# Mixture-of-experts stage of a two-part network: token blocks of 32 on quarters of the array instead of 64 on halves

## The chip, the cores and the metric

The kernel runs on one core of a Trainium2 chip. Engines by the profile's names: PE is the matrix engine (TensorE), PEld its weight loads, DVE the vector engine, ACT the scalar engine, POOL GpSimd, SP the engine that here only issues transfers. The metric is the device time of one execution in microseconds (us); lower is better. Before the change, three executions took 3697.03, 3705.31 and 3705.87 us, median 3705.31.

## The reference

The reference is a long float32 network for 512 tokens of 1024 channels: a recurrent token mixer with a Fourier branch, a mixture of experts, and two attention layers. Only the mixture of experts is touched:

```python
logits = h @ w_router + b_router                  # 512 tokens, 32 experts
top_val, top_idx = lax.top_k(logits, 4)           # each token goes to 4 experts
# for each expert e and the tokens that chose it:
u = xb @ w1[e] + b1[e]                            # 1024 -> 2048
glu = jnp.minimum(u[:, 0::2], 7.0)
lin = jnp.clip(u[:, 1::2], -7.0, 7.0)
act = glu * jax.nn.sigmoid(1.702 * glu) * (lin + 1.0)
y = act @ w2[e] + b2[e]                           # 1024 -> 1024
```

The gates weight the four results of a token and they are summed. One expert's w1 is 8 MB and its w2 is 4 MB, so the stage reads 402.65 MB of weights. The 2048 assignments are spread over the experts very unevenly. With the reference's own inputs and router, experts 0 to 31 get 44, 173, 113, 53, 8, 58, 162, 39, 48, 26, 50, 21, 51, 17, 79, 21, 70, 52, 73, 42, 159, 35, 36, 87, 96, 69, 135, 57, 66, 55, 46 and 7 tokens.

## The kernel before

**Routing (`settle`, from line 1386).** DVE turns the router's result into a count per expert (lines 1553 to 1558), a rank of every assignment within its expert, and a list that says which token stands in which row of which block (lines 1566 to 1577; the last product, on PE, is line 1477). `nblki` holds the number of blocks of each expert, one more than the number of multiples of 64 that its count exceeds. Here that makes 48 blocks. This chain is serial, and nothing of the expert stage's PE work starts before its list is there.

**The expert stage (`experts`, from line 1589).** A block is up to 64 tokens (`HT`) of one expert. All weights are loaded in pieces of 1 MB (line 1621, SP's queue) into a ring of 20 places (`RING`); an expert is 12 pieces, eight of w1 and four of w2, in the order of use. Nine of the first pieces are already loaded during `settle`, eleven more when the stage starts (line 1625). Piece n+20 is asked for when piece n has been used for the last time, that is in the last block of its expert (`used`, line 1620). A piece of w1 is two groups of 128 rows by one half of the columns, with runs of 4 KB.

For each block PE does, in this order: two bias products (line 1685, one ahead of each half of the first layer), 8 pieces of the first layer and 4 of the second (line 1698), two turns of the activations (line 1704) and one turn of the next block's rows (lines 1672 and 1674). A piece is four matmuls of 512 columns in float32. The tokens are the stationary operand, 64 columns wide, so that two matmuls run side by side on the two column halves of the array. The trace shows each float32 matmul as two instructions, so a block has 96 instructions of line 1698. DVE forms the activation (`swiglu`, lines 1791 to 1798) for one half while PE works on the next pieces. ACT computes the sigmoid and copies everything that is turned (lines 1748 to 1774), then writes the block's result with two transfers (line 1744). POOL gathers the next block's rows by their indices (line 1643), after PE has turned the present ones (`turned`), and makes the selector of the bias (line 1652).

Loops run over experts and, within them, over the expert's number of blocks, which each engine reads from `nblki` (line 1608). Whether the block is an expert's first or a later one, it runs the same instructions and the same waits. Within a block the second layer stands behind the first of the same block.

After the stage, `combine` (from line 1805) gathers four result rows for each token.

Of the kernel before, what the change touches and what calls it, by code (L numbers as in the profile page):

```python
# [57 lines left out]
MAXB = 64  # L58


def constants():
# [11 lines left out]
        "edges": np.broadcast_to(64.0 * np.arange(1, 9)[None, :], (P, 8)),  # L73
        "token": P * np.arange(TT)[None, :] + p,
        "headrow": (p % 32) == np.arange(8)[None, :],
        "halves": (p // 64) == (f // 64),
# [1309 lines left out]
def settle(nc, A, ps, T, R, M, N, spill, rows_in, raw_in, stored, kmt):  # L1386
# [6 lines left out]
    with stage(nc, "b_in", "var_ready", "root_ready", "scaled", "normed", "taken", "h_ready", "kept", "saved", "turned", "ht_out", "high", "pool_step",  # L1393
# [20 lines left out]
        def _(pool):  # L1414
# [9 lines left out]
            for i in (1, 3):  # L1424
                lo = slice(E * i, E * i + E)
                done(pool.tensor_tensor(M["b12"][lo, :], N["b1r"][lo, :], M["b12"][lo, :].bitcast(F32), ALU.subtract))

        @block.tensor
        def _(pe):
# [46 lines left out]
            for j in range(JK):  # L1476
                last = pe.matmul(ps[0:64, 7, 0:MAXB], R["who"][:, j, :], R["where"][:, j, :], start=(j == 0), stop=(j == JK - 1))
# [3 lines left out]
        def _(act):  # L1481
# [17 lines left out]
            act.activation(M["b12"][:, :], N["b1r"][:, :], ACT.Copy).then_inc(high, 1)  # L1499
# [10 lines left out]
        def _(dve):  # L1510
# [55 lines left out]
            done(dve.scalar_tensor_tensor(out=R["row"][:, :], in0=R["blk"][:, :], scalar=64.0, in1=R["rank"][:, :], op0=ALU.mult, op1=ALU.add))  # L1566
            done(dve.tensor_copy(T["slot"][:, :], R["row"][:, :]))
            done(dve.tensor_tensor(R["over"][:, 0:JK, :], bc(R["rank"][:, :], 2, 8), bc(S("edges"), 1, JK), ALU.is_ge))
            done(dve.tensor_reduce(R["low"][:, :], R["over"][:, 0:JK, :], AX_X, ALU.add))
            done(dve.tensor_tensor(R["blk"][:, :], R["blk"][:, :], R["low"][:, :], ALU.add))  # L1570
            done(dve.scalar_tensor_tensor(out=R["low"][:, :], in0=R["low"][:, :], scalar=-64.0, in1=R["rank"][:, :], op0=ALU.mult, op1=ALU.add))
# [7 lines left out]

def piece_source(A, e, s):  # L1580

    w1 = A["w1"][0, e].rearrange("(k p) n -> p k n", p=P)
    w2 = A["w2"][0, e].rearrange("(k p) n -> p k n", p=P)
    if s < 8:
        return w1[:, 2 * (s % 4):2 * (s % 4) + 2, (s // 4) * D:(s // 4 + 1) * D]
# [1474 lines left out]
```

## Time and profile before

| | us |
|---|---|
| median of three executions (lowest, highest) | 3705.31 (3697.03, 3705.87) |
| span of the profiled execution | 3706.0 |
| expert stage on PE (first to last matmul of line 1698) | 979.6 to 2151 |
| PE busy over the span | 3295.0 (89%) |
| PE idle in the expert stage, waiting for weights | 27.2 |
| loads of 1 MB from w1 and w2 | 384 |
| mean transfer rate in most of the expert stage | 369 to 399 GB/s |

The page divides the span in 40 slices of 92.65 us; the expert stage is slices 11 to 24. In them PE is busy nearly all the time and DVE and ACT are nearly idle, while the transfer engines are at nine tenths or more in most slices. The profile's own execution stands at the median of the timed ones, so sums made against its span carry over.

### The profile page before, as it was taken

To read this page: it belongs to the slowest core of one execution; us is meant where nothing else is said; L and a number is where in the kernel's file an instruction comes from. 1 tells how busy PE (TensorE), PEld (TensorE's weight loads), DVE (VectorE), ACT (ScalarE), POOL (GpSimd) and SP (SyncE) were. 2 spreads that over 40 slices of the span, in tenths; PEclk is the share of its full clock that TensorE was granted. 3 is DMA by queue.
4 is the path that set the end of the run, shared out by engine and by line. 5 is a ranking of instruction groups with operands and counts; after the bars stand their busy time and mean duration, and the time that the engine had idled before them with its cause. 6 is when DMAs were issued, how large, how long until landed. Compare 5 with 4: busy or idle time off the path is not lost. (4 is left out here: it accounts for less than half of the span.)

```text
span 3706.0 us, 63217 instructions
## 1 busy us (share of the span) xinstructions
PE 3295.0 (89%) x25517; PEld 2108.3 (57%) x25518; DVE 1399.2 (38%) x2384; ACT 984.3 (27%) x1766; POOL 154.3 (4%) x221
## 2 busy tenths in 40 slices
PE   3998788787799997999999969987899899878998
PEld 2878677676433332333333327865578778655787
DVE  5535545546211111111111146544643365446433
ACT  2333313312111111111111103343532233435321
POOL 0000000000300000000000010000000000000000
PEclk8999889888799999999999989997999999979999
DMA  6621320324789999998986944331033133310331
GB/s 217 237 97 33 98 94 8 98 71 157 298 297 396 366 400 399 396 397 320 397 312 244 385 172 122 99 49 35 1 93 101 45 115 101 47 35 1 94 100 57
DMA packets 273124, 647.39 MB, mean 175 GB/s; under 512 B 36890, under 2 KB 97050, under 8 KB 270978
## 3 DMA queue, kind: packets, MB, share of 16 engines
q1 hardware_dynamic: 251314, 605.12, 45.6%
q0 software_dynamic: 6224, 21.24, 1.8%
q10 hardware_dynamic: 15360, 17.82, 1.5%
q8 instruction: 167, 2.74, 0.3%
q14 instruction: 59, 0.48, 0.0%
HBM read 600.85 MB, written 43.27 MB: 174 GB/s over the span
## 5 line engine op out<-in xcount | busy, mean ns | idle before, releaser
L1698 PE MATMUL ps<-raw,ex_xT 128*64 128x512 f32 x3072 | 698.0, 599 | 21.8 <-DMA raw<-in_w_dram 21.7
L1698 PEld LDWEIGHTS ps<-raw,ex_xT 128*64 128x64 f32 x3072 | 206.6, 137 | 419.2 <-issue 375.9
L1791 DVE TENSOR_SCALAR ex_gl<-ps 128x256 f32<-128x256 f32 x96 | 40.8, 425 | 1014.4 <-PE ps L1698 1014.4
L1698 PE MATMUL ps<-raw,ex_aT 128*64 128x512 f32 x1536 | 350.8, 596 | 6.1 <-DMA raw<-in_w_dram 5.5
L1698 PEld LDWEIGHTS ps<-raw,ex_aT 128*64 128x64 f32 x1536 | 105.3, 137 | 205.0 <-issue 187.5
L1950 PE MATMUL ps<-zhi,hh 128*128 128x512 f32 (+1 forms) x448 | 169.8, 379 | 0.4 <-DVE hl L2080 0.4
L1951 PE MATMUL ps<-zlo,hh 128*128 128x512 f32 (+1 forms) x448 | 169.0, 377 | 0.0
L1952 PE MATMUL ps<-zhi,hl 128*128 128x512 f32 (+1 forms) x448 | 168.6, 376 | 0.0
L2497 PE MATMUL ps<-uu_hi,hh 128*128 128x512 f32 x384 | 151.9, 395 | 12.2 <-DVE uu_lo L2609 12.2
L2499 PE MATMUL ps<-uu_hi,hl 128*128 128x512 f32 x384 | 152.2, 396 | 0.0
L2498 PE MATMUL ps<-uu_lo,hh 128*128 128x512 f32 x384 | 152.0, 396 | 0.0
L2609 DVE TENSOR_TENSOR uu_lo<-u_raw,uu_hi 128x2048 fp32r<-128x2048 f32 x30 | 68.6, 2292 | 202.7 <-ACT uu_hi L2575 202.7
L1765 ACT ACTIVATE ex_aT<-ps 128x256 f32<-128x256 f32 x96 | 36.8, 383 | 406.4 <-PE ps L1704 406.4
L2497 PE MATMUL ps<-uu_hi,u_oh 128*128 128x512 f32 x320 | 126.7, 396 | 0.4 <-DVE u_ol L2614 0.4
L2071 DVE TENSOR_TENSOR zlo<-oT,zhi 128x1024 fp32r<-128x1024 f32 (+1 forms) x64 | 74.6, 1166 | 137.2 <-ACT zhi L1987 136.5
L2498 PE MATMUL ps<-uu_lo,u_oh 128*128 128x512 f32 x320 | 126.3, 395 | 0.0
L2499 PE MATMUL ps<-uu_hi,u_ol 128*128 128x512 f32 x320 | 126.3, 395 | 0.0
L1987 ACT ACTIVATE zhi<-oT 128x1024 fp32r<-128x1024 f32 (+1 forms) x64 | 64.9, 1014 | 215.5 <-PE ps L1952 155.6
L1759 ACT ACTIVATE ex_arow<-ex_gl 128x256 f32<-128x256 f32 x96 | 40.0, 417 | 300.1 <-DVE ex_gl L1791 300.1
L2575 ACT ACTIVATE uu_hi<-u_raw 128x2048 fp32r<-128x2048 f32 x30 | 57.3, 1915 | 213.2 <-PE ps L2499 207.2
L2307 ACT ACTIVATE za<-ps,nsa_nm 128x256 f32<-128x256 f32 (+3 forms) x160 | 81.1, 511 | 109.0 <-DVE nsa_nm L2331 109.0
L2270 PE MATMUL ps<-small,za 128*128 128x128 f32 x544 | 86.1, 291 | 16.2 <-DVE za L2342 16.2
(558 smaller groups left out, 6018.8 us busy)
## 6 DMA issues: line engine op xcount, KB each, us to landing
raw<-in_w_dram SPq DMA_DIRECT2D x384, 1024.0 KB, 19.3
oT<-in_w_in_dram SPq DMA_DIRECT2D x64, 512.0 KB, 3.6
u_raw<-in_w_in_dram SPq DMA_DIRECT2D x24, 1024.0 KB, 5.2
expert_out<-xn SPq DMA_DIRECT2D x4, 4096.0 KB, 16.8
expert_out<-ex_yrow ACTq DMA_DIRECT2D x98, 128.0 KB, 6.4
late_ada<-in_w_ada_dram SPq DMA_DIRECT2D x12, 1024.0 KB
early_w<-in_w_in_dram SPq DMA_DIRECT2D x10, 1024.0 KB, 6.6
mT<-in_w_ada_dram SPq DMA_DIRECT2D x4, 2048.0 KB, 19.9
```

The costliest lines, as they stand in the source:

```text
L1698: mm = pe.matmul(o, x, M["raw"][:, (slot + LATE_SLOTS) % RING, k, h * 512:(h + 1) * 512], start=(s >= 8 and kk == 0), stop=(kk == 7))
L1950: pe.matmul(o, x_hi, w_hi, start=(kk == 0), stop=False)
L1951: pe.matmul(o, x_hi, w_lo, start=False, stop=False)
L1952: last = pe.matmul(o, x_lo, w_hi, start=False, stop=(kk == KD - 1))
L1987: act.activation(hi[q % nh][cut], raw[q % nr][cut], ACT.Copy).then_inc(hi_done, 1)
L2071: dve.tensor_tensor(lo[q % nh][cut], raw[q % nr][cut], hi[q % nh][cut].bitcast(F32), ALU.subtract).then_inc(lo_done, 1)
L2270: mm = pe.transpose(ps[:, 4 + x, b * P:(b + 1) * P], Z["p"][:, i % NB, x, b * P:(b + 1) * P], S("ident"))
L2307: act.activation(Z["p"][:, i % NB, x, 0:u["n"]], ps[:, (i % 2) * 2 + x, 0:u["n"]], ACT.Exp, bias=Z["nm"][:, i % 4, x:x + 1], accum_out=Z[" ...
L2497: pe.matmul(o, x_hi, w_hi, start=first, stop=False)
L2498: pe.matmul(o, x_hi, w_lo, start=False, stop=False)
L2499: return pe.matmul(o, x_lo, w_hi, start=False, stop=last)
L2609: dve.tensor_tensor(lo[q % nh], raw[q % nr], hi[q % nh].bitcast(F32), ALU.subtract).then_inc(lo_done, 1)
```

## The change

`HT` becomes 32: a block has up to 32 tokens, and its matmuls have 32 stationary columns and run on four column quarters. A first-layer piece is now one group of 128 rows of w1 with all 2048 columns (8 KB runs), four matmuls of 512 columns, one for each quarter, all into one bank. In the second layer a quarter takes 256 of the 1024 result columns: a piece is eight matmuls of 256 columns. Each expert has at least two blocks and otherwise one for each begun 32 tokens. PE's order changes too: first layer of block w, turn of block w-1's activations, turn of block w+1's rows, second layer of block w-1. An expert's first block is a copy of the code of its own, with the waits for the pieces; later blocks have none. `swiglu` and the sigmoid run once a block. The result goes out with four transfers of 32 rows by 256 columns instead of two of 64 by 512.

```diff
-MAXB = 64
+MAXB = 128
+HT = 32
+EDGES = SEQ // HT
@@ settle, SP @@
-            b1 = A["b1"][0].rearrange("e (p h n) -> h e p n", p=2, h=2)
-            for i in range(4):
-                sp.dma_start(N["b1r"][E * i:E * i + E, :].rearrange("e (p n) -> e p n", p=2), b1[i // 2]).then_inc(b_in, 16)
+            for j in range(4):
+                sp.dma_start(N["b1r"][E * j:E * j + E, :], A["b1"][0][:, j * 512:(j + 1) * 512]).then_inc(b_in, 16)
@@ settle, POOL @@
-            for i in (1, 3):
-                lo = slice(E * i, E * i + E)
-                done(pool.tensor_tensor(M["b12"][lo, :], N["b1r"][lo, :], M["b12"][lo, :].bitcast(F32), ALU.subtract))
+            done(pool.tensor_tensor(M["b12"][:, 1, :], N["b1r"][:, :], M["b12"][:, 0, :].bitcast(F32), ALU.subtract))
@@ settle, PE @@
-                last = pe.matmul(ps[0:64, 7, 0:MAXB], R["who"][:, j, :], R["where"][:, j, :], start=(j == 0), stop=(j == JK - 1))
+                last = pe.matmul(ps[0:HT, 7, 0:MAXB], R["who"][:, j, :], R["where"][:, j, :], start=(j == 0), stop=(j == JK - 1))
@@ settle, DVE (and HT, EDGES for 64 and 8 in the lines after) @@
-            done(dve.tensor_tensor(R["over"][:, :, :], bc(cnt, 2, 8), bc(S("edges"), 1, E), ALU.is_gt))
+            done(dve.tensor_tensor(R["over"][:, :, :], bc(cnt, 2, EDGES), bc(S("edges"), 1, E), ALU.is_gt))
             done(dve.tensor_reduce(R["nblk"][:, :], R["over"][:, :, :], AX_X, ALU.add))
+            done(dve.tensor_scalar(R["nblk"][:, :], R["nblk"][:, :], 1.0, None, ALU.max))
+            done(dve.tensor_copy(R["nblki"][:, 0, :], R["nblk"][:, :]))
             done(dve.tensor_scalar(R["nblk"][:, :], R["nblk"][:, :], 1.0, None, ALU.add))
-            done(dve.tensor_copy(R["nblki"][:, :], R["nblk"][:, :]))
+            done(dve.tensor_copy(R["nblki"][:, 1, :], R["nblk"][:, :]))
@@ piece_source @@
-    if s < 8:
-        return w1[:, 2 * (s % 4):2 * (s % 4) + 2, (s // 4) * D:(s // 4 + 1) * D]
-    return w2[:, 2 * (s - 8):2 * (s - 8) + 2, :]
+    if s < 8:
+        return A["w1"][0, e].rearrange("(k p) (a n) -> p k a n", p=P, a=2)[:, s, :, :]
+    return A["w2"][0, e].rearrange("(h k p) n -> p k h n", p=P, h=2)[:, s - 8, :, :]
@@ experts, SP: reload @@
-                    sp.wait_ge(used, w * NP + s + 1)
+                    if s < W1P:
+                        sp.wait_ge(used1, w * W1P + s + 1)
+                    else:
+                        sp.wait_ge(used2, w * W2P + s - W1P + 1)
@@ experts, PE @@
+            def bias(w):
+                pe.wait_ge(picked, w + 1)
+                pe.matmul(ps[:, WIDE, :], M["pick"][:, :], M["b12"][:, 0, :], start=True, stop=False)
+                pe.matmul(ps[:, WIDE, :], M["pick"][:, :], M["b12"][:, 1, :], start=False, stop=False).then_inc(bias_done, 1)
+            def first_layer(w, i, g, fresh):
+                pe.wait_ge(x_out, w + 1)
+                for s in range(W1P):
+                    if fresh:
+                        landed(i, g + s)
+                    for j in range(4):
+                        mm = pe.matmul(ps[HT * j:HT * j + HT, WIDE, :], M["xT"][:, s, :], M["raw"][:, place((g + s) % NS), j // 2, (j % 2) * 512:(j % 2) * 512 + 512],
+                                       start=False, stop=(s == W1P - 1))
+                    mm.then_inc(used1, 1)
+            def second_layer(w, i, g, fresh):
+                pe.wait_ge(y_out, w + 1)
+                pe.wait_ge(at_out, w + 1)
+                for s in range(W2P):
+                    if fresh:
+                        landed(i, g + W1P + s)
+                    for half in range(2):
+                        for n in range(4):
+                            mm = pe.matmul(ps[HT * n:HT * n + HT, OUT, 0:256], M["aT"][:, 4 * half + s, :],
+                                           M["raw"][:, place((g + W1P + s) % NS), half, n * 256:(n + 1) * 256],
+                                           start=(s + half == 0), stop=(s + half == W2P))
+                    mm.then_inc(used2, 1)
+            def one_block(i, g, before, fresh):
+                w = now()
+                pe.wait_ge(emptied, w)
+                bias(w)
+                first_layer(w, i, g, fresh)
+                turn_act(w - 1)
+                turn_rows(w + 1)
+                second_layer(w - 1, i, before, before == g)
+                pe.reg_add(r, r, 1)
+            def expert(i, e, g):
+                one_block(i, g, g - NP, True)
+                with pe.Fori(0, later_blocks_of(pe, e)) as _:
+                    one_block(i, g, g, False)
@@ experts, ACT @@
-                for h in range(2):
-                    act.dma_start(rows_out[bass.ds(at_row, HT), h * 512:(h + 1) * 512], M["yrow"][HT * h:HT * h + HT, :]).then_inc(written, 16)
+                for n in range(4):
+                    act.dma_start(rows_out[bass.ds(at_row, HT), n * 256:(n + 1) * 256], M["yrow"][HT * n:HT * n + HT, :]).then_inc(written, 16)
+            def body():
+                w = now()
+                act_out(w)
+                rows_turned(w + 2)
+                sigmoid(w + 1)
+                rows_back(w)
+                act.reg_add(r, r, 1)
```

## Rows read from the trace of the kernel before

**Rows 1.** Stretches of the expert stage: length, busy us (instructions), granted clock, transfer share, rate
```profile
core 0: us, PE busy (x) PEld busy (x) DVE busy (x) ACT busy (x) POOL busy (x), PEclk, DMA share, GB/s
1100.00:1200.00 100.00, 100.00 (x472) 33.92 (x468) 12.99 (x32) 17.59 (x29) 6.07 (x12) 1.00 1.02 388
...
1400.00:1500.00 100.00, 82.62 (x356) 24.17 (x354) 11.37 (x28) 12.65 (x22) 4.95 (x10) 0.98 1.03 399
```
**Rows 2.** Waits from 980 to 2150: who for whom, us in total, times, longest
```profile
PE ps L1698 <- DMA raw<-in_w_dram: 27.2, 40, 2.0
```
**Rows 3.** PE in order of time, one undisturbed block: start us, us, group, count
```profile
1568.24 0.51 PE L1685 MATMUL ps<-ex_b,ex_pick 128*128 128x512 f32 x1
1568.68 5.37 PE L1698 MATMUL ps<-raw,ex_xT 128*64 128x512 f32 x24
1573.98 0.44 PE L1704 MATMUL ps<-small,ex_arow 128*128 128x128 f32 x2
...
1576.11 3.60 PE L1698 MATMUL ps<-raw,ex_aT 128*64 128x512 f32 x16
1579.65 0.44 PE L1704 MATMUL ps<-small,ex_arow 128*128 128x128 f32 x2
...
1584.40 0.50 PE L1685 MATMUL ps<-ex_b,ex_pick 128*128 128x512 f32 x1
```
**Rows 4.** Weight loads in order of time where matmuls of 32 columns run on quarters
```profile
412.75 0.13 PEld L1149 LDWEIGHTS ps<-late_ada,cpad 128*32 128x32 f32 x4 [0.30 <-issue]
413.18 0.13 PEld L1149 LDWEIGHTS ps<-late_ada,cpad 128*32 128x32 f32 x4 [0.30 <-issue]
```
**Rows 5.** PE in order of time, quarters with only 128 columns
```profile
2535.01 0.27 PE L2142 MATMUL ps<-oT,za 64*32 64x128 f32 x2
...
2535.12 0.27 PE L2142 MATMUL ps<-oT,za 64*32 64x128 f32 x2
```
**Rows 6.** Costliest PE groups by line: busy us, mean ns, idle before
```profile
L2287 PE MATMUL ps<-za,zb 128*64 128x128 f32 x960 | 79.7, 301 | 0.0
```
**Rows 7.** Transfer queues from 1500 to 1600: packets, MB, share of 16 engines
```profile
q1 hardware_dynamic: 9767, 37.65, 96.2%
q0 software_dynamic: 320, 1.05, 3.9%
q10 hardware_dynamic: 640, 1.05, 2.8%
```
**Rows 8.** The same from 104 to 108, packets of 17 KB
```profile
DMA packets 96, 1.67 MB, mean 418 GB/s; under 512 B 0, under 2 KB 0, under 8 KB 0
```
**Rows 9.** PE in four stretches of 5 us: length, busy, granted clock, transfer share, rate
```profile
1425.00:1430.00 5.00, 2.96 (x12) 0.89 1.04 349
1430.00:1435.00 5.00, 4.74 (x18) 0.77 1.04 401
...
1440.00:1445.00 5.00, 4.12 (x20) 1.00 1.03 412
```
**Rows 10.** Routing's end in order of time
```profile
953.76 0.42 DVE L1553 TENSOR_TENSOR rt_over<-ps,small 128x256 f32<-128x256 f32 x1 [0.85 <-PE ps L1469]
...
954.89 0.18 DVE L1556 CAST nblki<-rt_nblk 128x32 int32<-128x32 f32 x1
...
962.48 1.23 DVE L1575 TENSOR_TENSOR rt_where<-small,rt_blk 128x1024 f32<-128x1024 f32 x1
963.76 3.67 PE L1477 MATMUL ps<-rt_where,rt_who 128*64 128x64 f32 x32 [9.26 <-DVE rt_where L1575]
```
**Rows 11.** Gather of the block's rows, POOL in order of time
```profile
1582.02 0.94 POOL L1643 DMA_INDIRECT ex_xrow<-expert_in,ex_index  x1 [0.77 <-POOL ex_index L1649]
```
**Rows 12.** The same gathers, from issue to landing, over the stage
```profile
DMA to landing us min/median/max: 3.6/6.9/8.1
```
**Rows 13.** ACT around a block's turns and its writes
```profile
1580.12 0.38 ACT L1765 ACTIVATE ex_aT<-ps 128x256 f32<-128x256 f32 x1 [2.92 <-PE ps L1704]
...
1584.51 0.60 ACT L1774 ACTIVATE ex_yrow<-ps 128x512 f32<-128x512 f32 x1 [3.00 <-PE ps L1698]
```

More of the change, by code:

```diff
@@ L72, in constants @@
         "causal": np.where(f <= p, 0.0, NEG),
-        "edges": np.broadcast_to(64.0 * np.arange(1, 9)[None, :], (P, 8)),
+        "edges": np.broadcast_to(float(HT) * np.arange(1, EDGES + 1)[None, :], (P, EDGES)),
         "token": P * np.arange(TT)[None, :] + p,
         "headrow": (p % 32) == np.arange(8)[None, :],
-        "halves": (p // 64) == (f // 64),
+        "quarters": (p // 32) == (f // 32),
         "eye32": (p % E) == np.arange(E)[None, :],
@@ L1498, in _ @@
             act.wait_ge(b_in, 64)
[L1499 removed]
+            act.activation(M["b12"][:, 0, :], N["b1r"][:, :], ACT.Copy).then_inc(high, 1)
             act.wait_ge(logit, 1)
@@ L1592, in experts, with counter, later_blocks_of, every_block_but_one @@
     NP, NS, EU = 12, RING, RING // int(np.gcd(RING, 12))
-    HT = 64
-    TURNED, ROWS_T = 5, 3
-    WIDE = (0, 1)
-    OUT = 2
-    with stage(nc, "used", "indexed", "picked", "bias_done", "turned", "x_out", "biased", "mixed", "sig", "acted", "at", "at_out",
+    W1P, W2P = 8, 4
+    TURNED, ROWS_T, WIDE, OUT = 5, 3, 0, 2
+    with stage(nc, "used1", "used2", "indexed", "picked", "bias_done", "turned", "x_out", "biased", "emptied", "mixed", "sig", "acted", "at", "at_out",
                "y_out", "written") as (
-            block, used, indexed, picked, bias_done, turned, x_out, biased, mixed, sig, acted, at, at_out, y_out, written):
-        def counter(eng, name, first=0):
+            block, used1, used2, indexed, picked, bias_done, turned, x_out, biased, emptied, mixed, sig, acted, at, at_out, y_out, written):
+        def counter(eng, name):
             r = eng.alloc_register(name)
-            eng.reg_mov(r, first)
-            return r, lambda top=MAXB - 1: eng.snap(r, min_val=first, max_val=top)
+            eng.reg_mov(r, 0)
+            return r, lambda top=MAXB - 1: eng.snap(r, min_val=0, max_val=top)
         def blocks_of(eng, e):
-            return eng.value_load(R["nblki"][0:1, bass.ds(e, 1)], min_val=1, max_val=SEQ // HT)
+            return eng.value_load(R["nblki"][0:1, 1, bass.ds(e, 1)], min_val=2, max_val=EDGES)
+        def later_blocks_of(eng, e):
+            return eng.value_load(R["nblki"][0:1, 0, bass.ds(e, 1)], min_val=1, max_val=EDGES - 1)
+        def every_block_but_one(eng, body):
+            with eng.Fori(0, later_blocks_of(eng, 0)) as _:
+                body()
+            with eng.Fori(1, E) as e:
+                with eng.Fori(0, blocks_of(eng, e)) as _:
+                    body()
+        def place(slot):
+            return (slot + LATE_SLOTS) % RING
         @block.sync
@@ L1662, in _ @@
             r, now = counter(pe, "pe_blocks")
-            pe.sem_inc(used, NP)
             pe.sem_inc(turned, 1)
@@ L1731, in _ @@
-            turn_rows(0)
-            with pe.Fori(0, E // EU) as i:
-                for j in range(EU):
-                    expert(i, j)
-            for j in range(E % EU):
-                expert(E // EU, j)
+            def bias(w):
+                pe.wait_ge(picked, w + 1)
+                pe.matmul(ps[:, WIDE, :], M["pick"][:, :], M["b12"][:, 0, :], start=True, stop=False)
+                pe.matmul(ps[:, WIDE, :], M["pick"][:, :], M["b12"][:, 1, :], start=False, stop=False).then_inc(bias_done, 1)
@@ new lines, in turn_act @@
+            def turn_act(w):
+                pe.wait_ge(acted, w + 1)
+                for i2 in range(2):
+                    mm = pe.transpose(ps[:, ROWS_T, i2 * P:(i2 + 1) * P], M["arow"][:, i2 * P:(i2 + 1) * P], S("ident"))
+                mm.then_inc(at, 1)
+            def second_layer(w, i, g, fresh):
[10 more added lines that the diff above has]
+                    mm.then_inc(used2, 1)
@@ new lines, in _ @@
+            turn_rows(0)
+            bias(0)
+            first_layer(0, 0, 0, True)
+            turn_rows(1)
+            pe.reg_add(r, r, 1)
+            with pe.Fori(0, later_blocks_of(pe, 0)) as _:
+                one_block(0, 0, 0, False)
+            whole = (E - 1) // EU
+            with pe.Fori(0, whole) as i:
+                for j in range(EU):
+                    expert(i, i * EU + (j + 1), NP * (j + 1))
+            for e in range(1 + whole * EU, E):
+                expert(0, e, NP * e)
@@ L1738, in _ @@
+            w = now(MAXB)
+            turn_act(w - 1)
+            second_layer(w - 1, 0, NP * (E - 1), False)
         @block.scalar
```

169 lines of the change are left out of this document (61 added, 108 removed).

## Prediction

> **What bounds the kernel now.** I read the page's slices first: the expert stage is slices 11 to 24 of 40, with PE at nine tenths or ten and the transfer engines nearly as full. So two things compete, and the stretches of the stage say which one wins where [rows 1]: from 1100 to 1200 PE is busy 100.00 of 100 us at full clock with 388 GB/s beside it; from 1400 to 1500 it is busy 82.62 us while the transfer share is 1.03 and the rate 399 GB/s. The first kind of stretch is PE-bound, the second is load-bound. The waits give the sum: in all, PE sat idle for weights for only 27.2 us [rows 2]. The stage lasts 979.6 to 2151 = 1171.4 us. The change touches this stage and the end of routing; everything after is the same code.
>
> One block, from one bias product to the same one of the next block, runs from 1560.79 to 1584.40 = 23.61 us; the rows show its later part [rows 3]. Matmuls of line 1698 come in pairs on the two halves, 4 instructions in 0.857 us (24 from 1568.68 to the turn at 1573.98, 5.30 us, of which about 0.16 is filling). So 96 instructions take 20.57 us. The rest, 3.04 us, is the array emptied and filled again around other shapes: a bias product 0.59 each (twice), the first turn 0.53, the second turn with the row turn 1.32. 48 blocks x 23.61 = 1133.3 us, and 1171.4 - 1133.3 = 38 us is what waiting adds (27.2 of it plainly idle, the rest refilling and the slow clock at a few waits).
>
> The loads: from 1500 to 1600 with four blocks [rows 7], the shares of the queues add to 102.9%. The weight queue's part is 96.2 / 102.9 = 93.5 us for 37.65 MB, 2.60 us for a piece of 1 MB. A block's gather and write take (3.9 + 2.8) / 102.9 / 4 = 1.63 us; I use 1.67, as the stretch of 1400 to 1500 gives. An expert of one block takes the loads 12 x 2.60 + 1.67 = 32.9 us, PE 23.6.
>
> **A check of how the two combine.** I carry two sums through the 32 experts with the counts of the reference: loads one after another, no piece before the one 20 places earlier was used in its expert's last block; PE block by block, no first-block piece before it has landed. With the numbers above this gives an end of PE at 2151.6 (the trace: 2151), 38.7 us of waiting, and 107 us in which the loads stand because the ring is full. The long experts (3 blocks, 71 us of PE against 35 of loads) fill the ring and stop the loads; the run of short ones after them empties it and PE waits, above all at experts 11 to 14. I use the same two sums for the change.
>
> **PE's work per block.** First layer: 32 matmuls are 64 instructions, 4 at a time on quarters. The trace has this shape: 4 weight loads every 0.43 us with matmuls of 512 columns [rows 4]. 16 x 0.429 = 6.86 us, half of the 13.7 of before, for half the tokens. Second layer: 64 instructions of 256 columns, which no row shows. From below, quarters with 128 columns come 4 in 0.11 us [rows 5], so streaming, not issue, sets the pace, and 256 columns should take 0.214 for 4: 3.43 us. From above, matmuls of 128 columns on halves cost 79.7 / 960 = 0.083 us each where streaming alone would be 0.053 [rows 6]; at 0.083 each the layer is 5.3 us. I take 3.43, since rows 5 have the same quarters. Bias: one excursion, 0.59 + 0.22 for the second product = 0.81. Turns: one excursion, 1.32 as before, since line 1674 is issue-bound and not shortened. Sum 0.81 + 6.86 + 1.32 + 3.43 = 12.42 us for 32 tokens.
>
> **Blocks.** Counts up to 64 give two blocks, also the six experts with 32 or fewer; ceil(count / 32) beyond. Sum 87. PE: 87 x 12.42 = 1080.5 us against 1133.3, 52.8 less. Experts of one block go from 23.6 to 24.8, those with 65 to 96 tokens (seven) from 47.2 to 37.3, expert 2 (four blocks) from 47.2 to 49.7, the four of three blocks from 70.8 to 62.1 (five) or 74.5 (six).
>
> **What could wait within 12.42 us.** The second layer needs the turned activations: ACT's copy ended 0.85 us after the turn began [rows 3, 13], and the row turn covers 1.16. The gather follows the row turn: it is issued 2.4 us after the turn of the activations began and takes at most 8.1 to land [rows 3, 11, 12], 10.5 in all, and the next row turn begins 0.4 + 12.4 = 12.8 after; half as many rows. If this cover were gone, each us beyond would cost 87 us less the 49 of waiting. ACT issues four writes instead of two, about 2.3 us after the copy of the result [rows 13], with the next turn 7 us away. SP's queue waits for the second layer of an expert's last block, which now stands behind the next expert's first-layer pieces; these 8 are in the ring already (12 + 8 = 20), so it is 4 pieces late by one first layer and the sums hold it. I cost all of these at nothing.
>
> **Loads.** A w1 piece has runs of 8 KB in place of 4. Packets of 17 KB moved 1.67 MB in 4 us, 418 GB/s [rows 8]; the weight queue does 37.65 / 93.5 = 403. I take 2.50 us for a w1 piece (419 GB/s), 2.60 for w2; the bounds are 2.60 and 2.45. Gather and write per block: half the bytes but smaller writes; 0.9 us, from 0.7 to 1.3. An expert of two blocks: 8 x 2.50 + 4 x 2.60 + 1.8 = 32.2 us against PE's 24.8.
>
> **The clock.** Before, a starved PE had its waits spread over all 12 pieces. A wait of 2.04 us near 1426 took the granted clock to 0.89 and 0.77 in the next stretches, while waits of some 0.6 us each left it at 1.00 [rows 9]. Now a piece is used in 0.86 us and lands every 2.5, so a starved first layer waits 1.6 us at each piece: I expect 1.2 GHz there and 3 us more per such expert (bounds 0 and 5), nine times, 27 us.
>
> **The sum.** The two sums with these numbers: PE 1080.5, waiting 48.8, clock 27, the last second layer's turn 1.2: 1157.5 us against 1172.0, so -14.5. Where the ring is empty (experts 9 to 14) the stage goes at the loads' 32.2 us an expert; where five or six blocks come (1, 6, 20, 26, also 2) PE falls behind and the loads stand for 115 us. That is where the saved PE time goes: the floor by the loads alone would be some 115 us lower.
>
> Routing's end is on the path [rows 10]: the list product gets 128 moving columns instead of 64 at half clock, 3.67 to about 6.9 (+3.2); `rt_where` doubles (+1.1), the two `rt_who` steps halve (-1.2), the edges double (+0.8), two small operations (+0.4): +4.4. Two more writes at the end +1, more code to fetch +1. Total -14.5 + 6.4 = -8.1: span 3697.9, and since the span stands 0.7 above the median, 3697.
>
> **One rule against it.** The weight loads of the four quarters overlap each other and the matmuls: 4 of them take 0.13 us and recur every 0.43, which is streaming alone [rows 4]. By the Trainium skill, "TensorE: Matmul & The Clock Gate", Part 3, a weight load overlaps running matmuls only when its row group differs, and column quarters share theirs. The trace disagrees. Taken at its word it would add 0.13 to each of 32 groups of a block, rival B with 4.2 us.
>
> **Rivals.**
> A, loads gain nothing and starve PE as now: w1 pieces at 2.60. The stage then is 1178.9, +6.9; total +13: 3719. For: the steady rate may be a limit of all 16 engines. Against: rows 8.
> B, slower: a group of quarters doesn't reach streaming pace in the second layer. At 5.3 us the block is 14.3, PE 1244 with hardly a wait left: stage +90, 3800. It decides from about 0.5 us a block, where the two sums give no gain at all. For: rows 6, and 4.2 us by the rule gives more, near 4000. Against: rows 5.
> C, faster: the clock holds and block traffic is small (0.8, w1 2.45, block 12.1): stage -46, 3665. For: waits of 0.6 us left it at 1.00. Against: 2.04 did not.
> D, the gather lands over 2.3 us later than its longest or another hand-over is late, 1 us a block: stage +28, 3740. Against: rows 12.
>
> **Chances.** Forecast 0.44, A 0.20, B 0.08, C 0.16, D 0.12. What this kernel's measurement can tell from no change is about 0.3%, 11 us: below 3694 is faster, above 3716 slower. Half of the forecast's own range (3680 to 3714) is below 3694. Faster: half of 0.44 + C, and a little of A: 0.41. Slower: B, D, over half of A: 0.29. Same 0.30. The range reaches from C to D: 3662 to 3748.
>
> **What would show it.** Right: 87 blocks; bias to bias 12.4 us where nothing waits; second-layer weight loads 4 in 0.21; PE busy near 1080 us of the stage and waiting 50 to 75; clock under 1.00 at experts 9 to 14; slices above 410 GB/s. Wrong: a period of 14 (B), idle on the gather or on ACT's copy (D), the weight queue still at 403 (A), clock at 1.00 throughout (C).

## The result, and the profile after

The changed kernel takes 3733.0 us (median of four executions, 3728.2 to 3739.7) against 3705.6 us for the kernel before on the same chip: ratio 1.0074, 95% interval 1.0062 to 1.0087. The forecast was 3697. The profiled execution's span is 3734.3 us, against 3706.0.

The stage, from the first bias product to the end of the last second-layer matmul, lasts 1197.8 us (983.98 to 2181.8) against 1172.2 (978.78 to 2151.0): +25.6 of the +28.3 us by which the spans differ. The rest, +2.7, lies outside the stage. When the stage starts differs by up to 18 us between the profiled executions of the kernels below (965.6 to 984.0), and that difference is already there at routing's `rt_over` (937.0 to 957.0). So below I compare the stage's length, not where it ends.

The same two stretches as in [rows 1], changed kernel:

```profile
1100.00:1200.00 100.00, 97.19 (x1108) 40.45 (x1104) 12.84 (x32) 11.66 (x32) 11.64 (x24) 1.00 0.88 340
1400.00:1500.00 100.00, 84.20 (x862) 31.68 (x858) 9.63 (x24) 8.75 (x24) 8.89 (x18) 0.90 1.02 401
```

The kind of stretch is as before, but the granted clock of the second is 0.90 for 0.98. PE from 1046 on, one undisturbed block to hold against [rows 3]:

```profile
1046.85 0.50 PE L1694 MATMUL ps<-ex_b,ex_pick 128*128 128x512 f32 x1
...
1047.52 7.07 PE L1708 MATMUL ps<-raw,ex_xT 128*32 128x512 f32 x64
1054.53 0.44 PE L1716 MATMUL ps<-small,ex_arow 128*128 128x128 f32 x2
...
1055.66 3.66 PE L1728 MATMUL ps<-raw,ex_aT 128*32 128x256 f32 x64
1059.25 0.50 PE L1694 MATMUL ps<-ex_b,ex_pick 128*128 128x512 f32 x1
```

Bias to bias is 12.40 us; the forecast had 12.42. The 64 second-layer instructions run in 3.6 us, the forecast's streaming pace (3.43) and some filling. There are 87 blocks; at 12.40 each they are 1078.8 us of PE. So the work of PE is what was forecast. The waits of PE in the stage are not:

```profile
PE ps L1708 <- DMA raw<-in_w_dram: 33.3, 30, 1.8
PE ps L1694 <- issue: 29.0, 5, 6.0
PE ps L1708 <- issue: 12.3, 5, 2.5
```

The first line answers to [rows 2] (27.2 before). The two "issue" lines have no counterpart there: ten idle times in which PE waited for nothing that the profile shows, five ahead of a bias product and five within the first layer behind it. This is PE in order of time around the first pair:

```profile
1198.88 0.50 PE L1694 MATMUL ps<-ex_b,ex_pick 128*128 128x512 f32 x1
...
1207.69 3.66 PE L1728 MATMUL ps<-raw,ex_aT 128*32 128x256 f32 x64
1217.40 0.79 PE L1694 MATMUL ps<-ex_b,ex_pick 128*128 128x512 f32 x1 [6.05 <-issue]
1217.98 0.63 PE L1695 MATMUL ps<-ex_b,ex_pick 128*128 128x512 f32 x1
1218.54 1.94 PE L1708 MATMUL ps<-raw,ex_xT 128*32 128x512 f32 x8
1222.92 9.02 PE L1708 MATMUL ps<-raw,ex_xT 128*32 128x512 f32 x56 [2.44 <-issue]
...
1236.59 0.50 PE L1694 MATMUL ps<-ex_b,ex_pick 128*128 128x512 f32 x1
```

The block before takes 1217.40 - 1198.88 = 18.52 us and the next 19.19, for 12.40 each: 12.9 us more, of which 8.5 are the two idle times and 4.4 the slower clock after them (8 matmuls in 1.94 us instead of 1.07). The other four pairs stand at 1414, 1586, 1785 and 1960; measured in the same way they cost 11.6, 12.1, 11.9 and 11.7 us. These five places are where PE's outer loop over five experts turns back. Together that is some 60 us of PE's time (the expectations below take 12.9 for each, the largest of the five); part of it comes back, since the loads go on meanwhile.

What is transferred in the stage (985 to 2150) by the instruction queue, packets of 16 KB, kernel before first, then changed:

```profile
q8 instruction: 6, 0.10, 0.0%
```

```profile
q8 instruction: 83, 1.36, 0.5%
```

I read this so: the kernel before brings its loop's instructions once and keeps them, and the changed one brings them again at each turn. The queue's row doesn't say which engine its packets are for; the experiments decide. The changed kernel's PE loop holds, for each of five experts, the block twice (the first block with waits for its pieces, and a later one), ten copies of 282 matrix instructions and weight loads (64 + 64 + 13 pairs of them); before it was five copies of 222.

The weight queue from 1500 to 1600 [rows 7]:

```profile
q1 hardware_dynamic: 6836, 38.59, 96.2%
q10 hardware_dynamic: 1325, 0.90, 2.8%
q0 software_dynamic: 288, 0.79, 2.5%
```

With the 0.6% of the instruction queue the shares add to 102.1; the weight queue's part is 94.2 us for 38.59 MB, 410 GB/s; from 1400 to 1500 the same working gives 407. Before it was 403. A piece is 2.56 to 2.58 us on average; the forecast had 2.53 (2.50 for w1). A block's gather and write are 5.3 / 102.1 of 100 us over about six to seven blocks, 0.8 us; the forecast had 0.9.

Routing's end [rows 10], and the stage's last turn of the activations on ACT and PE:

```profile
965.91 2.29 DVE L1576 TENSOR_TENSOR rt_where<-small,rt_blk 128x2048 f32<-128x2048 f32 x1
...
968.26 5.79 PE L1476 MATMUL ps<-rt_where,rt_who 128*32 128x128 f32 x32 [10.48 <-DVE rt_where L1576]
```

```profile
2172.99 0.44 PE L1716 MATMUL ps<-small,ex_arow 128*128 128x128 f32 x2
2173.21 0.38 ACT L1791 ACTIVATE ex_yrow<-ps 128x256 f32<-128x256 f32 x1 [3.01 <-PE ps L1728]
2173.77 1.75 ACTq L1773 DMA_DIRECT2D expert_out<-ex_yrow  x4
2175.92 0.38 ACT L1786 ACTIVATE ex_aT<-ps 128x256 f32<-128x256 f32 x1 [2.32 <-issue]
...
2176.45 5.35 PE L1728 MATMUL ps<-raw,ex_aT 128*32 128x256 f32 x64 [3.01 <-ACT ex_aT L1786]
```

At the very end no next block's work stands between the turn and the second layer. ACT copies the result, issues four writes (1.75 us) and only then copies the turned activations: PE waits 3.0 us and then runs for a while at the slower clock (5.35 us for 3.66), 4.7 us in all.

### The profile page after: what moved, and what is told of

Same layout as the page of the kernel before. It is cut to its first block and busy times, and to the rows that moved or that the text cites. A ratio compares the mean times of both kernels' runs of the same rounds, so it can differ in the third digit from the quotient of the medians.

```text
span 3734.3 us, 78487 instructions
## 1 busy us (share of the span) xinstructions
PE 3274.6 (88%) x32456; PEld 2181.9 (58%) x32457; DVE 1383.1 (37%) x2350; ACT 916.2 (25%) x1779; POOL 206.7 (6%) x337
## 5 line engine op out<-in xcount | busy, mean ns | idle before, releaser
L1708 PE MATMUL ps<-raw,ex_xT 128*32 128x512 f32 x5568 | 649.6, 615 | 45.6 <-DMA raw<-in_w_dram 33.3
L1708 PEld LDWEIGHTS ps<-raw,ex_xT 128*32 128x32 f32 x5568 | 173.9, 112 | 474.4 <-issue 403.6
L1728 PE MATMUL ps<-raw,ex_aT 128*32 128x256 f32 x5568 | 321.5, 383 | 3.0 <-ACT ex_aT L1786 3.0
L1728 PEld LDWEIGHTS ps<-raw,ex_aT 128*32 128x32 f32 x5568 | 173.0, 110 | 113.3 <-issue 5.8
L1791 ACT ACTIVATE ex_yrow<-ps 128x256 f32<-128x256 f32 x87 | 33.5, 385 | 266.1 <-PE ps L1728 266.1
```

Source lines behind the costliest of these rows:

```text
L1708: mm = pe.matmul(ps[HT * j:HT * j + HT, WIDE, :], M["xT"][:, s, :], M["raw"][:, place((g + s) % NS), j // 2, (j % 2) * 512:(j % 2) * 512 + ...
L1728: mm = pe.matmul(ps[HT * n:HT * n + HT, OUT, 0:256], M["aT"][:, 4 * half + s, :], M["raw"][:, place((g + W1P + s) % NS), half, n * 256:(n ...
```

## Experiments

The theory, F: the copies of PE's loop are too many bytes to be kept, so each turn back fetches them again and PE stands while the first come in. Its first rival, J: turning back costs in this loop whatever it holds. Each run's ratio is against the kernel before, measured beside it.

### PE's outer loop taken away

```diff
-            whole = (E - 1) // EU
-            with pe.Fori(0, whole) as i:
-                for j in range(EU):
-                    expert(i, i * EU + (j + 1), NP * (j + 1))
-            for e in range(1 + whole * EU, E):
+            for e in range(1, E):
                 expert(0, e, NP * e)
```

> The changed kernel with PE's 31 later experts written out one after another instead of six turns of a loop over five experts; the work is the same. Theory F (code fetch): the loop body, ten block copies, is some 180 KB of PE code and is not kept, so each of the five backward branches waits for its first code: the trace after shows 5 idle times of about 6.0 us and 5 of about 2.4 us, put down to issue, and slow clock behind them, 12.9 us a time against the 12.4 us period. Written out there is no backward branch over a long body: these idle times go, the time falls by 25 to 35 us (part of 64 us comes back as waits for weights) to about 3705, the code fetched stays near 86 packets in the stage. Rival G (the gaps are hand-overs of another engine, or the selector or gather at an expert's border): the gaps stay, 3733. Rival H (fetching any new code is the cost, not the branch): the time stays or rises, with the idle spread over all experts.

3708.2 us (3703.8 to 3714.8, ten executions), ratio 1.0008 [0.9998, 1.0017]; the stage is 1175.2 us, 22.6 shorter than in the changed kernel. Waits of PE in the stage, then its instruction queue:

```profile
PE ps L1708 <- DMA raw<-in_w_dram: 45.1, 40, 1.9
...
PE ps L1728 <- ACT ex_aT L1782: 3.0, 1, 3.0
```

```profile
q8 instruction: 72, 1.18, 0.4%
```

No wait for issue is left, though nearly as many instructions are fetched (72 packets for 83): in a straight line they are fetched ahead of PE. It is not the traffic that costs, but the standing still at the turn. The rivals G and H fall: the other engines and the work are the same, and the gaps are gone. Of the 41.3 us of idle time taken away, 11.8 come back as waits for weights. From 1400 to 1500, with no turn of the outer loop in it, the stretch is this:

```profile
1400.00:1500.00 100.00, 86.06 (x826) 30.26 (x822) 9.64 (x24) 8.72 (x24) 8.88 (x18) 0.85 1.02 403
```

Slower by 0.74% became slower by 0.08%: 24 us, the whole measured loss within the intervals. 1.18 MB for 62 copies of the block (those of all experts but the first) is about 19 KB for a copy, 67 bytes for each of its 282 instructions; by the same figure a copy of the kernel before is about 15 KB. My expectations say 18 and 14. Both are estimates: the packets may hold other engines' code too, and some of PE's may have come before 985. So every size below is given from the smaller figure to the larger.

### The turn back announced to the sequencer

```diff
-            with pe.Fori(0, whole) as i:
+            with nc.Fori(0, whole, engines=[mybir.EngineType.PE], hint_back_edge=True) as i:
```

> The changed kernel with a prefetch hint for the backward branch of PE's loop over five experts, nothing else. Theory F: the first code of the body is fetched before the branch, so the 6.0 us gaps shrink; the second gap of 2.4 us may stay. Between 3705 and 3720. Rivals G and H: 3733.

3727.4 us (3712.5 to 3732.9, five executions), ratio 1.0064 [1.0046, 1.0083]. In the profiled execution, the fastest of the five:

```profile
PE ps L1708 <- DMA raw<-in_w_dram: 33.8, 30, 2.1
PE ps L1708 <- issue: 16.4, 5, 4.1
PE ps L1694 <- issue: 9.1, 3, 3.2
```

The idle time falls from 41.3 to 25.5 us, the stage to 1187.1, and 81 packets are still fetched. The hint shortens the wait ahead of the bias product (9.1 us in all for 29.0), not the second one (16.4 for 12.3), and hardly a packet is saved. The median is above the 3705 to 3720 that I expected: this execution is 14 us faster than the next of the five, and the gain over the changed kernel is small, with intervals that overlap. So the run bears theory F out in what it does to the waits, not in the time.

### The kernel before, with ten experts in PE's loop instead of five

```diff
+    EP = 2 * EU
...
-            with pe.Fori(0, E // EU) as i:
-                for j in range(EU):
+            with pe.Fori(0, E // EP) as i:
+                for j in range(EP):
```

> The kernel before with PE's loop over ten experts a turn instead of five; the work is the same, the body grows from about 71 to 142 KB of code. Theory F: the body no longer stays, code packets in the stage rise from 6 to 30 or more, and the two backward branches (before experts 10 and 20) cost a gap of about 6 us each and slow clock: 13 us each of PE, of which the first is taken back from the waits for weights at experts 11 to 14: 3711 to 3720. Rival J (a backward branch by itself drains PE in the changed kernel, whatever the size of the body): the kernel before has five such branches without a gap, so this one has two fewer and stays at 3705.

3718.8 us (3713.5 to 3722.1, ten executions), ratio 1.0030 [1.0020, 1.0041]. Two rows of its waits, line 1686 being the bias product that opens the loop's body, and the instruction queue:

```profile
PE ps L1699 <- DMA raw<-in_w_dram: 25.2, 39, 2.1
...
PE ps L1686 <- issue: 7.8, 2, 3.9
```

```profile
q8 instruction: 32, 0.52, 0.2%
```

Fewer turns back, yet slower: only the size of the body has changed, and with it appear the fetching and the waits that the kernel before doesn't have. J falls for this loop; for the changed kernel's own loop it is decided by the run with two experts below. Here a turn costs one wait of 3.9 us where I expected 6, less than the 8.5 of the changed kernel.

### w1 pieces in runs of 4 KB again

```diff
-                sp.dma_start(M["raw"][:, place(slot), :, :], piece_source(A, ...)).then_inc(raw_in[slot], 16)
+                for h in range(2):
+                    sp.dma_start(M["raw"][:, place(slot), h, :], piece_source(A, ...)[:, h, :]).then_inc(raw_in[slot], 16)
```

The same is done to the first loads, and PE waits for both halves of a piece.

> The changed kernel with each piece loaded by two transfers of 512 KB, so that w1's runs are 4 KB again as in the kernel before; 8 KB runs are what this leaves out. The prediction's term (2.50 us for a w1 piece instead of 2.60) says that this costs up to 20 us: 3745 to 3753. The trace after says 38.40 MB in 96.3 of 102.0 shares from 1400 to 1500, 2.58 us a piece on average against 2.60 before, so a rival says that the runs are worth almost nothing: 3733 to 3738.

3748.5 us (3744.5 to 3755.7, four executions), ratio 1.0118 [1.0097, 1.0140]: 16 us slower than the changed kernel. The weight queue from 1400 to 1500:

```profile
q1 hardware_dynamic: 10468, 38.11, 97.4%
```

With the shares of the other queues (2.5, 2.4, 0.6, 0.1) that is 403 GB/s, the rate of before, for 407. So giving up the changed kernel's loads costs 16 us. How much of it the longer runs are worth isn't shown: this run also doubles the number of transfers, of w2 pieces too, and I can't part the two.

### The writes of a block issued one turn later (on the flat kernel)

```diff
                 act_out(w)
-                rows_turned(w + 2)
+                act.wait_ge(y_out, w + 1)
+                write(behind() * HT)
+                act.reg_mov(q, r)
+                rows_turned(w + 2)
                 ...
-                act.wait_ge(y_out, w + 2)
-                write(w * HT)
```

> The experts of PE written out flat, as in the run without an outer loop, and one thing more: ScalarE no longer issues the four row stores of block w right after it copied them, but a turn later, behind its act_out. Everything is computed as before. In the changed kernel and in the flat one the last act_out stands behind the issue of four stores (1.75 us) and the last second layer waits 3.0 us for it (ScalarE ex_aT), at the slower clock. Theory T (tail on the path, nothing else touched): the 3.0 us wait is under 0.5 us, stage from its first first-layer matmul 3 to 5 us shorter, 3704 us against 3708 of the flat one. Rival U (ScalarE's queue is needed mid stage): rows_turned, now behind the stores, comes 1.75 us later each block, x_out is waited for by PE in the blocks that do not wait for weights, a new wait 'ACT ex_xT' of up to 20 times 1 us, 3710 to 3725.

3700.3 us (3692.5 to 3712.1, twelve executions), ratio 0.9987 [0.9974, 0.9999]. The wait for ACT's copy is 1.1 us for 3.0, the stage 1171.4 us for 1175.2: 3.8 less, and no new wait appears mid stage. Theory T holds, though the wait isn't under 0.5 us as I expected of it: I take the remaining 1.1 us for the copy itself and the hand-over to it, as in an undisturbed block, where the turn of the rows covers it. The time is 8 us below the flat kernel's, more than the stage's 3.8, with intervals that just overlap.

### Experts of one block (with the late writes, flat)

```diff
-            done(dve.tensor_scalar(R["nblk"][:, :], R["nblk"][:, :], 1.0, None, ALU.max))
...
-                with pe.Fori(0, later_blocks_of(pe, e)) as _:
-                    one_block(i, g, g, False)
+                more = later_blocks_of(pe, e, 0)
+                pe.reg_mov(left, more)
+                with pe.If_ne(left, 0):
+                    with pe.Fori(0, more) as _:
+                        one_block(i, g, g, False)
```

PE's second layer now also has the waits for its pieces in every block, since the block before can be an expert's only one.

> The flat kernel with the late stores, and experts may have one block of 32 where they have at most 32 tokens; the changed kernel gives every expert at least two, so 6 of its 87 blocks are rows of nobody. Everything is computed. Theory G (PE's own time still bounds enough of the stage): 81 blocks in place of 87; by the recurrence over landings and blocks that fits the flat kernel the stage is 14 us shorter for it (not 6 x 12.4 = 74, since most of the removed blocks stand where PE waits for weights anyway), with the tail 3690 us. Rival H (the loads bound the stage where small experts stand): removed blocks turn into waits for weights one for one, 45 us of them become over 110 and the time is that of the run with late stores alone, 3704.

3686.0 us (3675.5 to 3696.7, six executions), ratio 0.9945 [0.9924, 0.9967]. The stage is 1156.8 us, 14.6 shorter than with late writes alone; 14 were expected for six blocks of 12.4 us less. Its waits:

```profile
PE ps L1708 <- DMA raw<-in_w_dram: 64.3, 55, 4.7
PE ps L1694 <- issue: 16.5, 4, 6.4
PE ps L1716 <- issue: 2.8, 1, 2.8
```

Theory G's numbers hold, and H's (over 110 us of waits, 3704) don't. Still, 60 of the 74 us are not gained. Of them 17 are more waits for weights and 19.3 are issue waits that come back; the rest is PE's slower clock and refilling, which no run parts (the granted clock from 1400 to 1500 is 0.76 for 0.85 in the flat kernel). The first of the issue waits:

```profile
1161.47 0.79 PE L1694 MATMUL ps<-ex_b,ex_pick 128*128 128x512 f32 x1 [6.02 <-issue]
```

This is the first block behind expert 4, which has 8 tokens, so that its copy for later blocks is jumped over. Counting blocks, the other three (at 1346.92, 1475.69 and 1551.47) stand behind experts 9, 13 and 15 and the one at line 1716 behind expert 31: five of the six experts with one block, and nowhere else. Behind expert 11 none is labelled so. A jump ahead over one copy can thus wait (1.4 to 6.4 us here) as a turn back does; that it waits for its instructions is the likely reading, but no run isolates it.

### The second layer between first-layer pieces 5 and 6

```diff
-                first_layer(w, i, g, fresh)
+                early = 6 if fresh else W1P
+                first_layer(w, i, g, fresh, range(early))
                 turn_act(w - 1)
-                turn_rows(w + 1)
+                if not fresh:
+                    turn_rows(w + 1)
                 second_layer(w - 1, i, before, True)
+                if fresh:
+                    first_layer(w, i, g, fresh, range(early, W1P))
+                    turn_rows(w + 1)
```

> As the kernel with one-block experts and late stores, and in an expert's first block PE does the second layer of the block before between pieces 5 and 6 of the first layer rather than behind piece 7. Everything is computed. PE waits for first-layer pieces in such blocks, 40 waits of about 1.1 us in the flat kernel; the second layer (3.66 us of work on pieces long there) would fill the wait for pieces 6 and 7. Theory W (waits in series with work that could fill them): 3 to 20 us shorter than the kernel without it. Rival X (loads bound): a second layer moved inside frees second-layer pieces a little earlier but first-layer pieces 6 and 7 3.7 us later, so the loads slip by as much as PE gains: within 3 us, or up to 5 longer since the turn of the rows also comes later and SwiGLU waits.

3677.6 us (3669.0 to 3686.8, six executions), ratio 0.9918 [0.9900, 0.9937]. The stage is 1151.3 us, 5.5 less than without it; the times differ by 8.4, with intervals that overlap. PE where it is starved:

```profile
1412.18 0.44 PE L1717 MATMUL ps<-small,ex_arow 128*128 128x128 f32 x2
1413.14 3.66 PE L1729 MATMUL ps<-raw,ex_aT 128*32 128x256 f32 x64 [0.52 <-issue]
1416.59 1.93 PE L1709 MATMUL ps<-raw,ex_xT 128*32 128x512 f32 x16
```

Pieces 6 and 7 (the last row, 16 matmuls) no longer wait: they landed during the second layer. In exchange a small wait stands ahead of it, 17.4 us over 32 blocks (0.5 us each). It is labelled "issue"; with no turn of the rows between, ACT's copy of the activations is what I take it for, but no row says so. Rival X's side shows too: PE waits for SwiGLU to empty the first layer's bank (5.9 us in 28 blocks, where there were 0.2), and for the next rows (13.0 us for 8.7). The small gain is on the side of theory W, at its low end. This is the fastest of all kernels run, 0.8% below the kernel before.

### How large a loop is kept

Four kernels place the limit. A loop over fewer experts needs the ring's used places to divide evenly, so the number of places changes with it; one line in the changed kernel sets both (places, experts in a loop; SP's loop over experts changes with it).

```diff
-    NP, NS, EU = 12, RING, RING // int(np.gcd(RING, 12))
+    NP, NS, EU = 12, 18, 3
```

> The changed kernel with its outer loop kept but the ring used to 18 places instead of 20, so that PE's loop holds three experts, not five: 6 block copies of about 18 KB of instructions, some 108 KB, where five experts are 180 KB. The loop turns back ten times, not five. Everything is computed. Theory F (code that is not there is fetched again at each turn only when the loop's body is too large to be kept): no waits for issue over 2 us at the branches, fewer than 25 instruction packets in the stage against 86. The two places fewer cost about 20 us by the recurrence of landings and blocks, so 3720 to 3735 us. Rival K (each backward branch of this loop costs, whatever the size): ten waits of 5 to 6 us, 20 us of places and 55 us of branches over the flat kernel, 3765 us or more.

3772.4 us (3765.6 to 3782.3, five executions), ratio 1.0178 [1.0157, 1.0198]. Here I was wrong, and the rival's number held:

```profile
PE ps L1694 <- issue: 51.1, 9, 5.9
PE ps L1708 <- DMA raw<-in_w_dram: 25.9, 24, 1.9
PE ps L1708 <- issue: 21.9, 9, 2.6
```

```profile
q8 instruction: 86, 1.41, 0.5%
```

Three experts in the loop, 108 to 114 KB, are not kept either. (The loop goes round ten times, so it turns back nine times, not ten.) Either the limit lies lower, or this kernel's loop is never kept. The next two differ only in the number of experts in the loop, two or three, at 12 places:

> The changed kernel with its outer loop kept, 12 places of the ring in use and two experts in PE's loop: 4 block copies of 18 KB, some 72 KB, as much as the whole loop of the kernel before. 15 backward branches. Everything is computed. With 12 places the loads run far less ahead, by the recurrence some 260 us are lost to waits for weights, near 3990 us; what counts is the difference to the run with three experts in the loop and the same 12 places. Theory S (a loop body is kept up to a size between 71 KB, which the kernel before keeps, and the 108 KB of three experts with 18 places, which were not kept): no waits for issue over 2 us at the branches and fewer than 30 instruction packets in the stage. Rival K (this kernel's code is never kept, since something other than its size, such as its two inner loops per expert, makes each branch back fetch): 15 waits of 5 us, over 80 packets.

> The changed kernel with 12 places of the ring in use and three experts in PE's loop: 6 block copies, some 108 KB, 10 backward branches. Everything is computed. Both theories expect what the run with 18 places showed: 9 or 10 waits of 5 to 6 us for issue and about 86 instruction packets. Theory S: slower than the run with two experts by 20 to 75 us (10 branches at up to 7.5, less what PE would have waited for weights anyway). Rival K: faster than the run with two experts, since it has 5 branches fewer, by 10 to 35 us.

Two experts: 3992.1 us (3987.7 to 3995.3, four executions). Three: 4025.5 us (4012.6 to 4034.7, four). The waits of the first and then of the second over the whole stage (960 to 2490), and the instruction queue (985 to 2440) of each:

```profile
PE ps L1708 <- DMA raw<-in_w_dram: 205.1, 191, 2.7
```

```profile
PE ps L1708 <- DMA raw<-in_w_dram: 145.5, 142, 2.9
PE ps L1694 <- issue: 56.1, 9, 6.8
PE ps L1708 <- issue: 22.4, 9, 2.6
```

```profile
q8 instruction: 8, 0.13, 0.0%
```

```profile
q8 instruction: 89, 1.46, 0.4%
```

With two experts (72 to 76 KB) the same code is kept: fifteen rounds, fourteen turns back, no wait for issue at any of them, 8 packets. With three it is fetched anew, 78.5 us of idle time, 33 us longer although it turns back nine times only. K falls, and J with it; the size decides. The last run is the kernel before with 18 places and six experts in PE's loop, 85 to 90 KB (the diff of the run with ten, and the line above):

> The kernel before with 18 places in use and six experts in PE's loop: some 85 KB of instructions, 5 turns; its own loop has five experts, 71 KB, and the loop of ten experts (142 KB) was fetched anew each turn (32 packets, 3.9 us for issue at each of two branches). Everything is computed. The two places cost 10 to 20 us by the recurrence, 3716 to 3726. Theory S leaves 85 KB open: kept (under 12 instruction packets in the stage, no issue wait at L1686) or not (about 27 packets and 4 issue waits of 4 us, 10 us more); it puts the limit in 71 to 85 or in 85 to 108 KB. Rival K expects no fetching in this kernel at any size under 142 KB.

3714.5 us (3710.5 to 3719.9, seven executions), ratio 1.0030 [1.0018, 1.0041]. That is put down to the two places less: PE's waits for weights are 39.0 us for 27.2, and no wait for issue stands in the stage. Its instruction queue from 985 to 2150:

```profile
q8 instruction: 7, 0.11, 0.0%
```

Kept, over four turns back. So a body of 85 to 90 KB was kept and one of 108 to 114 KB was not.

The Trainium skill, "Advanced Engine Details and Errata", section "ISA Cache", gives TensorE 128 KB in lines of 16 KB. The packets agree (1.41 MB / 86 = 16 KB). That a body of about 110 KB isn't kept does not: planned by the page's figure, three experts would have fitted. The Trainium skill, "Runtime: NRT & Kernel Launch", section "Instruction fetch mechanics", says that a long kernel needn't fit and that crossing from one block of instructions to the next is mostly hidden; the flat run agrees. The same section says that a taken branch whose target lies outside the current window of two pages must wait for a fetch. The turn back of the changed kernel (8.5 us idle) is such a wait, but a window of two 16 KB pages is not what the traces show: bodies of 71 to 90 KB turned back without one.

## Why the prediction was wrong

The direction was missed: -8.1 us forecast, +27.4 measured. That 3733 lies within the stated range, 3662 to 3748, is luck: it is between rivals A (3719) and D (3740), and neither is what happened. The failed step is one term of the sum, "more code to fetch +1". I took the added instructions for traffic and not for a loop that no longer stays in place. Removing the turns back gives 22.6 us of stage and 24 us of time. The trace of before had a row that bears on it (six instruction packets in the whole stage), but I asked for it only after the result; and I never multiplied the block's code by its copies in the loop: 5 x 222 instructions before, 10 x 282 after, by the estimates above from 71 to 75 KB to 180 to 190.

That term is not all. The flat kernel, which is without it, is at 1.0008 [0.9998, 1.0017] and not at the forecast's 3697: 17.7 us of its stage (1175.2 for 1157.5) are missed as well: the loads, the end and a part that stays unexplained.

Point by point:

- **PE's work: right.** 12.40 us a block (12.42), 3.6 us for the second layer (3.43 plus filling), 87 blocks. The quarters stream. The period also refutes rival B and the rule on weight loads that stood for it: there is no room for 0.13 us in each of 32 groups.
- **Waits for weights and clock: right in kind, too small in sum.** Beyond 87 undisturbed blocks the forecast had 48.8 + 27 + 1.2 = 77 us, the flat kernel has 96: 45.1 idle for weights, 3.2 idle elsewhere, and 48 of slower clock and refilling, which no run parts. The clock falls where PE is starved, as forecast (0.85 from 1400 to 1500 in the flat kernel), where rival C had it at 1.00; what it costs by itself was not measured.
- **Loads: right in sign, a third to three fifths of the size.** A piece went from 2.60 us to between 2.56 and 2.58, not to 2.53. My two sums with 2.58 give 1165.8 us for the stage instead of 1157.5: 8 us. The row of 418 GB/s that I leaned on was of 17 KB packets with no block traffic beside them; runs of 8 KB mixed with gathers reach 407 to 410. The truth lies about halfway between rival A, no gain at all, and my own value; the run with 4 KB runs in two transfers is back at 403 GB/s.
- **The end of the stage: missed, about 5 us.** "ACT issues four writes instead of two ... with the next turn 7 us away" was worked out for the middle of the stage. At the end no first layer stands before the last turn; the late writes took 3.8 us of it back.
- **Gather and hand-overs (rival D): right to cost nothing.** No wait on either over 0.2 us between the stage's first block and its end.
- **Routing's end: about right.** `rt_where` +1.06 (+1.1), the list product +2.12 (+3.2). From `rt_over` to the first bias product the two traces have 25.0 and 27.0 us, +1.9 for a forecast of +4.4 (whose terms add to 4.3). The +2.7 outside the stage says little, since its start moves by more than that.

Ledger of the stage: 1157.5 forecast; +8 for the pieces; +5 for the end; +22.6 for the turns back: 1193 of 1197.8. Some 5 us stay unexplained; the flat kernel shows the same gap, so they don't belong to the loop. How far the two sums can be trusted shows in the turns: with 12.9 us at each of the five they give 1196.1 for 1165.8, 30 us for what the runs measured as 22.6.

Why the flat kernel is no faster than the kernel before can be read from the same figures. PE's undisturbed work is 54 us less (1133.3 to 1078.8). Against it stand 21 us more of idle time (48.3 for 27.2) and 36 more of slower clock and refilling (48.1 for 11.7). Allowing experts of one block gives 14.6 back.

## What to carry to other kernels

Count the bytes of an unrolled loop body on each engine before a change multiplies its copies or its instructions: here bodies up to some 90 KB on PE turned back free of charge. In the changed kernel, bodies from some 110 KB on cost two idle times and a slower clock at every turn, about 12 us; in the kernel before, one of 142 to 150 KB cost one idle time of 3.9 us. Compare the number of instruction packets in the stage before and after, and idle time labelled "issue" at the line that opens the loop: that is the mark. Where the body can't be made smaller, writing it out flat costs nothing that these runs could see, though PE idled where it jumped over a copy.

## What the runs showed of the hardware that was not expected

- Instructions fetched in a straight line cost no visible wait: 72 packets, 1.18 MB, beside transfer engines that were nine tenths busy.
- A turn back to code that isn't there stops PE twice: 5.3 to 6.8 us in the kernels with five or three experts in the loop, then 2.4 to 2.6 us after ten matmul instructions, and those behind it run at the lower clock for part of a block (8 in 1.94 us for 1.07). In the kernel before with ten experts it is one wait of 3.9 us. Why the second appears only with the smaller matmuls isn't settled; the quarter matmuls use up instructions twice as fast (64 in 7 us for 24 in 5.3), which would fit, but no run isolates it.
- Behind a jump forward over one copy (about 19 KB) PE idled 1.4 to 6.4 us in four cases and 2.8 in a fifth.
- Four column quarters with 32-column weight loads run 64 matmul instructions of 256 columns in 3.6 us, where streaming alone is 3.43 by the forecast's working: the loads hide.
